# A hybrid RWKV-7 and pooling layer on one NeuronCore: some fp32 products of the time-mixing stage issued once per head, 64 stationary columns at a time

## The chip, the core and the metric

The kernel runs as one program on one core of a Trainium2 chip. The metric is device time in microseconds (us), the median of three runs. TensorE's clock has two levels, 1.2 and 2.4 GHz; the profile shows which one was granted.

Two things about the rows need saying once. A matrix product on TensorE is a pair of instructions: LDWEIGHTS puts the stationary operand into the array (PEld in the profile), MATMUL streams the moving operand past it (PE). And a product of two fp32 operands stands in the trace as two such pairs, so four products read "x8" on PE and "x8" on PEld; a product of two fp32r operands, and a transpose, stands as one pair. In a row, `128*128 128x64` means 128 active rows times 128 active (stationary) columns, and a moving operand of 64 columns; `128*64` would be 64 stationary columns. Column counts that repeat "128x" at the front count partitions first.

## The reference, cut to what matters

The layer normalises x, projects it with one large matrix, mixes the result over time in two branches, gates and merges them, projects again and adds an embedding. The change lies in branch A, the RWKV-7 recurrence of 16 heads of width 64, for a prompt of 256 tokens and 8 sample sequences of 8 tokens:

```python
def _wkv7_scan(S0, r, decay, k, v, a_vec, b_vec):
    # S_t = S_{t-1} diag(w_t) + (S_{t-1} a_t) b_t^T + v_t k_t^T ;  o_t = S_t r_t
    def step(S, inp):
        r_t, w_t, k_t, v_t, a_t, b_t = inp
        sa = jnp.einsum('bhij,bhj->bhi', S, a_t)
        S = S * w_t[..., None, :] + sa[..., :, None] * b_t[..., None, :] + v_t[..., :, None] * k_t[..., None, :]
        o = jnp.einsum('bhij,bhj->bhi', S, r_t)
        return S, o
...
    h = _rmsnorm(x, lw['norm_pre'])
    z = h @ lw['w_in']
...
    S, o = _wkv7_scan(wkv0, rh, decay.reshape(B, T, H, N), kh, vh, -kk, kk * ah)
...
    m = jax.nn.sigmoid(gate_a) * (y_a @ lw['w_branch'][0]) + jax.nn.sigmoid(gate_b) * (y_b @ lw['w_branch'][1])
    x = x + _rmsnorm(m @ lw['w_out'], lw['norm_post'])
    x = x + jax.nn.sigmoid(x @ lw['w_ple_gate']) * (p.astype(x.dtype) @ lw['w_ple'])
```

## The kernel before, in words

All 320 tokens (256 of the prompt, 64 of the samples) lie along the free dimension; channels lie on the 128 partitions. Every large weight matrix is split into a high and a low fp32r part (`wh`, `wl`, made by ACT and DVE from `wraw`), and each tile of 128 channels is made by `passes`: three products, wh by high, wh by low, wl by high, each with 320 or 328 moving columns. These are the rows of L1727, L1728 and L1729, in what follows the **stream**.

The recurrence is worked in 8 pairs of heads. A pair fills the 128 partitions, head 0 on rows 0 to 63 and head 1 on rows 64 to 127. The tokens are cut into G = 5 chunks of C = 64: four of the prompt (GP = 4), and one that holds the eight sample sequences. In a chunk the recurrence is a set of 64 by 64 matrix products for each head. To do both heads at once, the stationary operand is block diagonal: a tile such as `ABD`, `vBD` (also called `XBD`), `VtBD`, `kBD` (`SBD`) or `bBD` (`UBD`) holds for each chunk 128 columns, columns 0 to 63 with head 0's block on rows 0 to 63 and zeros below, columns 64 to 127 with head 1's block on rows 64 to 127 and zeros above. `flat(t, g)` gives these 128 columns.

`mix(r, q)` does the recurrence of pair r and, between its steps, the stream of pair q. `st.advance(n)` issues n steps of the stream (three products each), so that TensorE works while DVE, ACT and POOL prepare the next operand; the numbers in `AFTER` set by hand how many steps stand after which product. In the order of the program a pair's own products are:

- **sample states** (L1863): 8 products, one for each sample sequence, stationary `S0T`, moving `zr` with 80 columns;
- **scores** (L1869, L1874): 10 products with 128 moving columns, stationary `bBD` and `kBD`;
- `turned_keys`: 8 transposes;
- **inverse levels**, twice: `products(n)` (L1882: 4 products, stationary `ABD`, moving `Y`, 64 columns), three stream steps, `update(n)` (L1889: 4 products, stationary `XBD`, moving `Tm`, 64 columns), two stream steps. DVE masks the first result into `Tm`, and adds the second to `Y`;
- the **chain** over the four prompt chunks (L1915 to L1934), in which every product waits for DVE's result of the one before;
- **outputs** (L1945 to L1950): for each of the 5 chunks two or three products into one PSUM region, 14 in all, with 64 moving columns, and no stream between them; then a transpose, two wide products (L1958, L1959) and the mean (L1963).

Semaphores order the engines. The last product of each group tells the reader (`z_ps`, `t_ps`, `m_ps`, `o_ps`).

Of the kernel before, what the change touches and what calls it, by code (L numbers as in the profile page):

```python
# [30 lines left out]
P = 128  # L31
# [7 lines left out]
TB = 8  # L39
T = TP + NB * TB  # L40
TS = T + NB
C = 64
# [128 lines left out]
def build(nc, x_prompt, x_sample, state_wkv, state_shift, state_pool, p_prompt, p_sample, norm_pre, norm_post,  # L171
# [3 lines left out]
    with ExitStack() as ctx:  # L175
# [4 lines left out]
        def at(word, name, shape, dt=F32):  # L180
            size = int(np.prod(shape[1:])) * (2 if dt == BF16 else 4)
            used[name] = (word, word + (size + 3) // 4)
            return nc.alloc_sbuf_tensor_at(name, list(shape), dt, offset=base + 4 * word)
# [62 lines left out]
        ABD = r1.take("ABD", [P, G, 2, C])  # L246
# [4 lines left out]
        VtBD = r1.take("VtBD", [P, G, 2, C])  # L251
        ZaBD = r1.take("ZaBD", [P, 2, C])
        EndBD = r1.take("EndBD", [P, 2, C])
        S0T = r1.take("S0T", [P, NB, P])
        S0n = r1.take("S0n", [P, NB, C])
        S0D = r1.take("S0D", [P, NB, C])
        UBD, SBD, XBD = bBD, kBD, vBD
# [12 lines left out]
        ar = r1.take("ar", [P, 2, T])  # L270
        Y = r1.take("Y", [P, G, C])
        Tm = r1.take("Tm", [P, G, C])
        ARB = r1.take("ARB", [P, G, C])
        ARK = r1.take("ARK", [P, G, C])
# [6 lines left out]
        Zs = r1.take("Zs", [P, 2, C])  # L281
# [6 lines left out]
        zr = at(used["Y"][0], "zr", [P, NB, 2 * TB + C])  # L288
# [101 lines left out]
        x1h = at(used["hh"][0], "x1h", [P, KT * T], F32R)  # L390
        x1l = at(used["hl"][0], "x1l", [P, KT * T], F32R)
        end = max(b for _, b in used.values())
        room = (nc.sbuf_usable_end if not callable(nc.sbuf_usable_end) else nc.sbuf_usable_end())
        assert base + 4 * end <= room, (base + 4 * end, room)
# [5 lines left out]
        B01, B23, B45 = [ctx.enter_context(nc.psum_tensor(f"wide{i}", [P, 1024], F32)) for i in range(3)]  # L400
        B = [w[:, 512 * i:512 * (i + 1)] for w in (B01, B23, B45) for i in range(2)]
# [19 lines left out]
        def cfs(name):  # L421
            a, b = CF[name]
            return cf[:, a:b]
# [5 lines left out]
        ident, istk, ones2, meand = [cfs(n) for n in ("ident", "istk", "ones2", "meand")]  # L429

        def half(q):
            return slice(HD * q, HD * q + HD)
# [5 lines left out]
        def flat(t, g):  # L438

            return t[:, g].rearrange("p h c -> p (h c)")  # L440

        def tok(g):
            return slice(C * g, C * g + C)
# [1277 lines left out]
        def _(pe):  # L1721
            M = nc.tensor
# [21 lines left out]
            def transpose(out, in_):  # L1744
                rows = in_.shape[0]
                return M.transpose(out, in_, ident[0:rows, 0:rows])  # L1746


            pe.wait_ge(s["const_in"], 16)
            for _ in range(WARM):  # L1750
# [3 lines left out]
            for t in range(3):  # L1754
# [8 lines left out]
                for c in range(4):  # L1763
                    if t:
                        pe.wait_ge(s["hT_done"], 4 * (t - 1) + c + 1)
                    for k in range(4):
                        col = P * (4 * c + k)
                        last = M.matmul(B[c][:, P * k:P * k + n], rows_of[:, col:col + P], scales[0:n, t - 1, 0:n],
                                        start=True, stop=True) if t else transpose(B[c][:, P * k:P * k + n], rows_of[:, col:col + P])
# [46 lines left out]
            for j in range(1, CH_FIRST):  # L1816
# [8 lines left out]
                for n in [2 * k + m for k in MAP_TILES[j] for m in range(2)]:  # L1825
# [3 lines left out]
                             start=k == 0, stop=k == KT - 1).then_inc(s["xw_used"], 1)  # L1829
# [18 lines left out]
            def mix(r, q):  # L1848
# [11 lines left out]
                pe.wait_ge(s["dpl_ready"], r + 1)  # L1860
                pe.wait_ge(s["s0t_ready"], r * 2 + 2)
                for b in range(NB):
                    last = M.matmul(B45[:, P * b:P * b + 2 * TB + C], S0T[:, b, :], zr[:, b, :], start=True, stop=True)  # L1863
                last.then_inc(s["z_ps"], 1)

                pe.wait_ge(s["bbd_ready"], r * 2 + 2)
# [1 line left out]
                for g in range(G):  # L1868
                    last = M.matmul(B01[:, P * g:P * (g + 1)].rearrange("p (a c) -> p a c", a=2), flat(bBD, g),  # L1869
                                    ar[:, :, tok(g)], start=True, stop=True)  # L1870
                last.then_inc(s["score_ps"], 1)
                pe.wait_ge(s["bv_ready"], r + 1)
                for g in range(G):
                    last = M.matmul(B23[:, P * g:P * (g + 1)].rearrange("p (a c) -> p a c", a=2), flat(kBD, g),  # L1874
                                    ar[:, :, tok(g)], start=True, stop=True)
# [3 lines left out]
                def products(n):  # L1879
                    pe.wait_ge(s["y_ready"], r * (LEVELS + 1) + n + 1)  # L1880
                    for g in range(GP):
                        last = M.matmul(B[0][:, tok(g)], flat(ABD, g), Y[:, g, :], start=True, stop=True)  # L1882
                    last.then_inc(s["t_ps"], 1)

                def update(n):
                    pe.wait_ge(s["t_ready"], r * LEVELS + n + 1)
                    pe.wait_ge(s["x_ready"], r * (2 * LEVELS) + 2 * n + 2)
                    for g in range(GP):
                        last = M.matmul(B[1][:, tok(g)], flat(XBD, g), Tm[:, g, :], start=True, stop=True)  # L1889
                    last.then_inc(s["m_ps"], 1)  # L1890

                def turned_keys():
# [7 lines left out]
                for n in range(LEVELS):  # L1900
                    pe.wait_ge(s["ark_ready"], r * 5 + (3 if n == 0 else 5))
                    products(n)
                    st.advance(AFTER["product"])
                    update(n)
                    st.advance(AFTER["update"])
# [4 lines left out]
                for n in range(2):  # L1910
                    last = transpose(B[5][:, P * n:P * (n + 1)], tail4[:, n].rearrange("p h c -> p (h c)"))
                last.then_inc(s["tail_ps"], 1)

                for g in range(GP):
                    M.matmul(B[2][:, 0:C], flat(AKBD, g), Vs[:, g, :], start=True, stop=g == 0)  # L1915
                    if g == 0:
                        M.matmul(B[2][:, C:2 * C], flat(AKBD, G - 1), Vs[:, G - 1, :], start=True, stop=False)
                        last = M.matmul(B[2][:, C:2 * C], ZaBD[:, :, :].rearrange("p h c -> p (h c)"), istk, start=False, stop=True)
                    else:
                        pe.wait_ge(s["s_ready"], r * GP + g)  # L1920
                        last = M.matmul(B[2][:, 0:C], flat(aBD, g), Ss[:, g - 1, :], start=False, stop=True)
# [5 lines left out]
                    last = M.matmul(B[3][:, 0:C], flat(YBD, g), RHS[:, 0, :], start=True, stop=True)  # L1927
                    if g == 0:
                        last = M.matmul(B[3][:, C:2 * C], flat(YBD, G - 1), RHS[:, 1, :], start=True, stop=True)
# [11 lines left out]
                for g in range(G):  # L1941
                    if g == 1:
                        pe.wait_ge(s["sbd_ready"], r * 2 + 2)
                    o = B[4][:, tok(g)]
                    M.matmul(o, flat(VtBD, g), ARK[:, g, :], start=True, stop=False)  # L1945
                    if g == G - 1:
                        M.matmul(o, ident, Zs[:, 1, :], start=False, stop=False)
                    elif g:
                        M.matmul(o, flat(SBD, g - 1), ar[:, 1, tok(g)], start=False, stop=False)
                    last = M.matmul(o, flat(UBD, g), ARB[:, g, :], start=False, stop=True)  # L1950
                last.then_inc(s["o_ps"], 1)

                pe.wait_ge(s["endbd_ready"], r * 2 + 2)
# [29 lines left out]
            with pe.Fori(1, PAIRS) as q:  # L1983
                mix(q - 1, q)
            mix(PAIRS - 1, PAIRS)


# [35 lines left out]
            for k in range(8):  # L2023
                w = NB * BUF
                last = transpose(B[k // 4][:, w * (k % 4):w * (k % 4 + 1)], spt[:, P * k:P * (k + 1)])
# [151 lines left out]
```

## Time and profile before

| | us |
|---|---|
| median of 3 runs (range) | 1162.03 (1160.96 to 1163.07) |
| the profiled execution, its span | 1162.2 |
| TensorE busy with matmuls / with weight loads | 1143.0 / 1113.6 |
| VectorE (DVE) busy | 815.9 |
| ScalarE (ACT) busy | 524.9 |
| one pair of heads in the steady part | 63.9 |

The span is the time from the first to the last instruction of one profiled execution. A busy matmul row is not the time that a matmul costs: matmuls are pipelined, each row runs from its start until its results are out, and rows overlap. What a matmul costs is read from the starts: the distance from the start of one group to the start of the next. The first matmul of a stream after an fp32 group is shown starting early, while its weights are still loading: its distance to the next start is 0.23 us, where 0.147 is the rule; the 0.08 us between them belongs to the group before.

### The profile page before, as it was taken

What the parts mean: (1) busy time and instruction counts of PE and PEld (TensorE: products, weight loads), DVE (VectorE), ACT (ScalarE), POOL (GpSimd) and SP (SyncE); (2) the same over time, 40 slices, a digit from 0 to 9 for tenths busy, and PEclk for the clock granted to TensorE, in tenths of its full rate; (3) what the DMA queues carried; (4) which work ended last, traced back from release to release, by engine and by line L of the source; (5) the groups of instructions that cost most, each with busy time, mean ns of one, the idle gap of its engine ahead of it and who ended that gap; (6) DMA issues with size and microseconds to landing.
All of it is one profiled execution on the core that took longest, in us unless ns stands there. A gap on an engine that the chain in (4) does not pass through costs nothing.

```text
span 1162.2 us, 22008 instructions
## 1 busy us (share of the span) xinstructions
PE 1143.0 (98%) x7826; PEld 1113.6 (96%) x7826; DVE 815.9 (70%) x1727; ACT 524.9 (45%) x888; POOL 148.9 (13%) x251
## 2 busy tenths in 40 slices
PE   6999999999999999999999999999999999999998
PEld 6889999999999999999999999999999999989998
DVE  5979898889898898988679644444444487775442
ACT  5444645546474636455363333333333243354332
POOL 2322131204031121211050000000000500000000
PEclk9999999999999999999999999999999999999999
DMA  9714433434334334343464555545555975515551
GB/s 242 189 37 122 119 103 112 109 108 113 108 101 120 100 103 118 103 114 97 118 184 126 157 152 144 147 142 162 144 146 156 259 196 156 148 56 158 161 163 42
DMA packets 279707, 155.08 MB, mean 133 GB/s; under 512 B 7717, under 2 KB 275661, under 8 KB 279012
## 3 DMA queue, kind: packets, MB, share of 16 engines
q1 hardware_dynamic: 272528, 139.65, 43.2%
q0 software_dynamic: 6992, 14.87, 5.1%
q8 instruction: 25, 0.41, 0.2%
q14 instruction: 14, 0.11, 0.0%
q10 hardware_dynamic: 148, 0.04, 0.0%
HBM read 149.15 MB, written 5.61 MB: 133 GB/s over the span
## 4 chain that ended last, share of the span: by engine, by line
PE 89%; DVE 5%; DMA 3%; issue 2%; ACT 1%; SPq 0%; DVEq 0%; ACTq 0%
PE acc L1727 19%; PE acc L1728 18%; PE acc L1729 18%; PE wide L1729 5%; PE wide L1728 5%; PE wide L1727 5%; DVE wl L1085 2%; PE wide L1828 2%; PE wide L2112 1%; PE wide L1746 1%; DMA wraw<-in_w_out 1%; PE wide L1882 1%; PE wide L1863 1%; PE wide L1950 1%; DMA xt<-in_x_prompt 1%
## 5 line engine op out<-in xcount | busy, mean ns | idle before, releaser
L1085 DVE TENSOR_TENSOR wl<-wraw,wh 128x1024 fp32r<-128x1024 f32 x256 | 317.6, 1249 | 167.0 <-ACT wh L709 164.6
L709 ACT CAST wh<-wraw 128x1024 fp32r<-128x1024 f32 x256 | 266.9, 1048 | 217.8 <-PE acc L1729 125.7
L1727 PE MATMUL acc<-hh,wh 128*128 128x320 f32 (+1 forms) x1084 | 348.9, 322 | 2.4 <-DVE hl L1171 1.9
L1728 PE MATMUL acc<-hl,wh 128*128 128x320 f32 (+1 forms) x1084 | 336.5, 310 | 0.0
L1729 PE MATMUL acc<-hh,wl 128*128 128x320 f32 (+1 forms) x1084 | 335.9, 310 | 0.0
L1727 PEld LDWEIGHTS acc<-hh,wh 128*128 128x128 f32 x1084 | 204.4, 189 | 3.7 <-DVE hl L1171 2.4
L1728 PEld LDWEIGHTS acc<-hl,wh 128*128 128x128 f32 x1084 | 204.1, 188 | 0.3
L1729 PEld LDWEIGHTS acc<-hh,wl 128*128 128x128 f32 x1084 | 204.0, 188 | 0.0
L1727 PE MATMUL acc<-x1h,wh 128*128 128x320 f32 x256 | 81.0, 316 | 0.0
L1727 PE MATMUL acc<-mh,wh 128*128 128x320 f32 x256 | 79.4, 310 | 1.5 <-DVE wl L1085 1.5
L1729 PE MATMUL acc<-x1h,wl 128*128 128x320 f32 x256 | 79.1, 309 | 0.0
L1729 PE MATMUL acc<-mh,wl 128*128 128x320 f32 x256 | 79.1, 309 | 0.0
L1728 PE MATMUL acc<-ml,wh 128*128 128x320 f32 x256 | 79.1, 309 | 0.0
L1728 PE MATMUL acc<-x1l,wh 128*128 128x320 f32 x256 | 79.1, 309 | 0.0
L1729 PE MATMUL wide<-hh,wl 128*128 128x320 f32 x192 | 59.5, 310 | 0.0
L1728 PE MATMUL wide<-hl,wh 128*128 128x320 f32 x192 | 59.3, 309 | 0.0
L1727 PE MATMUL wide<-hh,wh 128*128 128x320 f32 x192 | 59.2, 308 | 0.0
L1727 PEld LDWEIGHTS acc<-mh,wh 128*128 128x128 f32 x256 | 48.1, 188 | 1.9 <-DVE wl L1085 1.8
L1728 PEld LDWEIGHTS acc<-x1l,wh 128*128 128x128 f32 x256 | 48.1, 188 | 0.2
L1727 PEld LDWEIGHTS acc<-x1h,wh 128*128 128x128 f32 x256 | 48.1, 188 | 0.2
L1728 PEld LDWEIGHTS acc<-ml,wh 128*128 128x128 f32 x256 | 48.1, 188 | 0.0
L1729 PEld LDWEIGHTS acc<-mh,wl 128*128 128x128 f32 x256 | 48.1, 188 | 0.0
(424 smaller groups left out, 2099.5 us busy)
## 6 DMA issues: line engine op xcount, KB each, us to landing
wraw<-in_w_in SPq DMA_DIRECT2D x160, 512.0 KB, 3.8
wraw<-in_w_branch SPq DMA_DIRECT2D x32, 512.0 KB, 3.9
wraw<-in_w_out SPq DMA_DIRECT2D x32, 512.0 KB, 4.6
wraw<-in_w_ple_gate SPq DMA_DIRECT2D x32, 512.0 KB, 4.1
xt<-in_x_prompt SPq DMA_DIRECT2D x2, 1024.0 KB, 6.8
S0n<-in_state_wkv POOLq DMA_DIRECT2D x64, 32.0 KB, 4.3
out<-so POOLq DMA_DIRECT2D x16, 128.0 KB, 3.6
xt<-in_x_prompt POOLq DMA_DIRECT2D x2, 1024.0 KB, 8.6
```

What stands on the lines that cost most here:

```text
L709: A.copy(wh[:, slot, :], wraw[:, slot, :]).then_inc(s["hi_ready"], 1)
L1085: V.tensor_tensor(wl[:, slot, :], wraw[:, slot, :], wh[:, slot, :].bitcast(F32), ALU.subtract).then_inc(s["lo_ready"], 1)
L1727: M.matmul(out[:, 0:width], wh[:, slot, wcol], hi, start=first, stop=False)
L1728: M.matmul(out[:, 0:width], wh[:, slot, wcol], lo, start=False, stop=False)
L1729: return M.matmul(out[:, 0:width], wl[:, slot, wcol], hi, start=False, stop=last)
L1746: return M.transpose(out, in_, ident[0:rows, 0:rows])
L1828: M.matmul(B[n % 2][0:RANK, 0:T], (lw1, la1)[n % 2][:, k, :], xw[:, n % 4, :], start=k == 0, stop=k == KT - 1).then_inc(s["xw_used"], 1)
L1863: last = M.matmul(B45[:, P * b:P * b + 2 * TB + C], S0T[:, b, :], zr[:, b, :], start=True, stop=True)
L1882: last = M.matmul(B[0][:, tok(g)], flat(ABD, g), Y[:, g, :], start=True, stop=True)
L1950: last = M.matmul(o, flat(UBD, g), ARB[:, g, :], start=False, stop=True)
L2112: last = M.matmul(B[i % 4][:, 0:T], embedding_weights(i)[:, P * k:P * (k + 1)], pT[:, k, :], start=k == 0, stop=k == 1)
```

## The change

A helper, `by_head`, issues a product as two: head 0's 64 stationary columns into PSUM partitions 0 to 63, then head 1's 64 columns into partitions 64 to 127, both with the same moving operand. It takes the place of the plain product for the sample states, both kinds of inverse-level products, and the outputs. The scores, the transposes, the chain, the wide products and the stream stay as they are. Waits and signals stay where they were; a group's signal goes with the last half of the last product.

```diff
+            def by_head(out, heads, rhs, start, stop):
+
+                for h in range(2):
+                    last = M.matmul(out[half(h)], heads[:, half(h)], rhs, start=start, stop=stop)
+                return last
...
-                    last = M.matmul(B45[:, P * b:P * b + 2 * TB + C], S0T[:, b, :], zr[:, b, :], start=True, stop=True)
+                    last = by_head(B45[:, P * b:P * b + 2 * TB + C], S0T[:, b, :], zr[:, b, :], True, True)
...
-                        last = M.matmul(B[0][:, tok(g)], flat(ABD, g), Y[:, g, :], start=True, stop=True)
+                        last = by_head(B[0][:, tok(g)], flat(ABD, g), Y[:, g, :], True, True)
...
-                        last = M.matmul(B[1][:, tok(g)], flat(XBD, g), Tm[:, g, :], start=True, stop=True)
+                        last = by_head(B[1][:, tok(g)], flat(XBD, g), Tm[:, g, :], True, True)
...
-                    M.matmul(o, flat(VtBD, g), ARK[:, g, :], start=True, stop=False)
+                    by_head(o, flat(VtBD, g), ARK[:, g, :], True, False)
                     if g == G - 1:
-                        M.matmul(o, ident, Zs[:, 1, :], start=False, stop=False)
+                        by_head(o, ident, Zs[:, 1, :], False, False)
                     elif g:
-                        M.matmul(o, flat(SBD, g - 1), ar[:, 1, tok(g)], start=False, stop=False)
-                    last = M.matmul(o, flat(UBD, g), ARB[:, g, :], start=False, stop=True)
+                        by_head(o, flat(SBD, g - 1), ar[:, 1, tok(g)], False, False)
+                    last = by_head(o, flat(UBD, g), ARB[:, g, :], False, True)
```

In the built program each half carries a tile of 128 rows by 64 columns of the array, at column 0 for head 0 and at column 64 for head 1; every plain product around it carries the whole array, 128 by 128. No instruction moves past another; DVE, ACT and SP have the same order as before.

On TensorE, around the first inverse level of a pair (`Y`, `Tm`, `ABD`, `vBD` as above, `acc<-` the stream, `cf` the identity of a transpose), before:

```order
L1746 MATMUL wide<-cf,kBD 128x128 x4
L1901 ISA
L1882 MATMUL wide<-Y,ABD 128x64 x4
L1727 MATMUL acc<-hh,wh 128x320
L1728 MATMUL acc<-hl,wh 128x320
```

and now:

```order
L1746 MATMUL wide<-cf,kBD 128x128 x4
L1907 ISA
L1751 MATMUL wide<-Y,ABD 64x64 x8
L1727 MATMUL acc<-hh,wh 128x320
L1728 MATMUL acc<-hl,wh 128x320
```

The four products became eight halves at the same place, between whole-array transposes and the whole-array stream.

On TensorE, at the start of a pair's outputs (`VtBD`, `bBD`, `kBD` stationary), before:

```order
L1729 MATMUL acc<-hh,wl 128x320
L1945 MATMUL wide<-ARK,VtBD 128x64
L1950 MATMUL wide<-ARB,bBD 128x64
L1945 MATMUL wide<-ARK,VtBD 128x64
L1949 MATMUL wide<-ar,kBD 128x64
L1950 MATMUL wide<-ARB,bBD 128x64
```

and now:

```order
L1729 MATMUL acc<-hh,wl 128x320
L1751 MATMUL wide<-ARK,VtBD 64x64 x2
L1751 MATMUL wide<-ARB,bBD 64x64 x2
L1751 MATMUL wide<-ARK,VtBD 64x64 x2
L1751 MATMUL wide<-ar,kBD 64x64 x2
L1751 MATMUL wide<-ARB,bBD 64x64 x2
```

Each product became two halves behind each other; the groups of one chunk still follow each other without anything between.

## Rows read from the trace of the kernel before

**Rows 1.** The page: busy times, the granted clock, the chain that ended last.

```profile
PE 1143.0 (98%) x7826; PEld 1113.6 (96%) x7826; DVE 815.9 (70%) x1727; ACT 524.9 (45%) x888; POOL 148.9 (13%) x251
...
PEclk9999999999999999999999999999999999999999
...
PE 89%; DVE 5%; DMA 3%; issue 2%; ACT 1%; SPq 0%; DVEq 0%; ACTq 0%
```

**Rows 2.** Who TensorE waited for, whole span: total us, times, longest.

```profile
PE wide L1746 <- DMA cf<-in_const_f: 6.4, 1, 6.4
PE wide L1746 <- DVE scales L1135: 2.7, 1, 2.7
PE acc L1727 <- DVE wl L1085: 2.1, 2, 1.5
```

**Rows 3.** Busy time of each engine in one pair; columns as the header says.

```profile
core 0: us, PE busy (x) PEld busy (x) DVE busy (x) ACT busy (x) POOL busy (x), PEclk, DMA share, GB/s
...
171.80:235.70 63.90, 63.81 (x460) 62.41 (x459) 55.77 (x156) 35.24 (x69) 11.97 (x21) 1.00 0.40 109
```

**Rows 4.** Timeline of TensorE in one pair: the first update between two streams.

```profile
493.30 0.31 PE L1729 MATMUL acc<-hh,wl 128*128 128x320 f32 x1
493.45 1.00 PE L1889 MATMUL wide<-Tm,vBD 128*128 128x64 f32 x8
494.26 0.39 PE L1727 MATMUL acc<-hh,wh 128*128 128x320 f32 x1
494.49 0.31 PE L1728 MATMUL acc<-hl,wh 128*128 128x320 f32 x1
```

**Rows 5.** Timeline of TensorE: second and last output product of a pair, then the wide ones.

```profile
512.80 0.39 PE L1950 MATMUL wide<-ARB,bBD 128*128 128x64 f32 x2
...
515.48 0.39 PE L1950 MATMUL wide<-ARB,bBD 128*128 128x64 f32 x2
...
515.82 1.02 PE L1958 MATMUL wide<-xpB,bBD 128*128 128x512 f32 x2
516.68 1.02 PE L1959 MATMUL wide<-xpK,VtBD 128*128 128x512 f32 x2
```

**Rows 6.** Timeline of TensorE: the sample states and the scores.

```profile
472.48 1.91 PE L1863 MATMUL wide<-zr,S0T 128*128 128x80 f32 x16
474.22 1.32 PE L1869 MATMUL wide<-ar,bBD 128*128 128x128 f32 x10
475.38 1.28 PE L1874 MATMUL wide<-ar,kBD 128*128 128x128 f32 x10
```

**Rows 7.** Weight loads by shape, whole span: busy us, mean ns.

```profile
L1882 PEld LDWEIGHTS wide<-Y,ABD 128*128 128x128 f32 x128 | 15.5, 191 | 3.1 <-DVE Y L1433 2.6 <-issue 0.5
...
L1828 PEld LDWEIGHTS wide<-xw,la 128*96 128x96 f32 x32 | 5.2, 163 | 3.4 <-DVE xw L1214 0.2
```

**Rows 8.** Timeline of TensorE: transposes, the last from 64 rows (row tile 64 by 128).

```profile
1006.13 0.59 PE L1746 MATMUL wide<-cf,pt 128*128 128x128 f32 x3
1006.65 0.41 PE L1727 MATMUL acc<-mh,wh 128*128 128x320 f32 x1
1006.90 0.31 PE L1728 MATMUL acc<-ml,wh 128*128 128x320 f32 x1
```

**Rows 9.** Timeline of TensorE: transposes, the last with 64 stationary columns.

```profile
1075.39 0.49 PE L1746 MATMUL wide<-cf,yo 128*128 128x128 f32 x3
1075.64 0.39 PE L1727 MATMUL acc<-x1h,wh 128*128 128x320 f32 x1
1075.87 0.31 PE L1728 MATMUL acc<-x1l,wh 128*128 128x320 f32 x1
```

**Rows 10.** Matmuls by shape, whole span: the third transposes of rows 8 and 9.

```profile
L1746 PE MATMUL wide<-cf,yo 128*64 128x128 f32 x16 | 4.4, 272 | 0.0
...
L1746 PE MATMUL wide<-cf,pt 64*128 64x64 f32 x2 | 0.6, 275 | 0.0
```

## The prediction

> **What bounds the kernel now.** I read the page first: TensorE has a matmul in flight for 1143.0 us of 1162.2, at the higher clock level (2.4 GHz) throughout, and the chain that ended last lies for 89% on it [rows 1]. Then who TensorE waited for: after 9 us of start-up loads the longest item is 2.1 us for split weights [rows 2]. Then one pair of heads in the steady part: of 63.9 us TensorE is busy 63.81, DVE 55.77, ACT 35.24 [rows 3]. So TensorE's own instruction stream sets the end, and each us cut from it comes off the time, as long as DVE's 55.8 us a pair stay below the pair's new length. The profiled span is 1162.2 us, the median 1162.03: the sum can be made against either.
>
> What must be read next is what limits TensorE inside the products that change. Busy rows don't say it, starts do. The update's four products: their start to the next stream row is 0.81 us, and that stream row is early by 0.08 (0.23 to its successor instead of 0.147), so 0.89 us, or 0.223 each [rows 4]. The outputs: 2.68 us from the second to the fourteenth product, twelve products, again 0.223 each [rows 5]. The sample states, 80 moving columns instead of 64: 1.74 us for eight, 0.218 [rows 6]. A product is two pairs of load and matmul, so a pair takes 0.112 us, and it is the same for 64 and for 80 moving columns. The matmul does not set it. Its streaming time is seen where it is long: the wide products with 512 columns start 0.86 us apart, 0.43 for one of the two matmuls, 0.84 ns a column [rows 5]; that makes 0.054 us for 64 columns and 0.067 for 80. What sets 0.112 us is the weight load of 128 columns; half of the time the array streams nothing.
>
> **The change part by part.** *Count.* A pair has 8 products of sample states, 16 of inverse levels, 14 of outputs: 38, in six groups (one, four, one). Before they cost 38 x 0.223 = 8.47 us a pair, 67.8 us for eight pairs. All of it lies on TensorE's path; nothing hides it.
>
> *A load of 64 columns.* Loads of 128 columns take 191 ns in the rows, of 96 columns 163: 0.875 ns a column [rows 7]. 64 columns less make the load 0.056 us shorter: 0.112 becomes 0.056. The half load is then as long as the 64-column stream. There are twice as many: four loads of 0.056 and four matmuls of 0.054 a product.
>
> *Side by side or in turn.* That is the open term, and the trace of before has no two neighbouring column tiles at work to show it. The bounds: if the two heads' halves, which sit in different columns of the array, load and stream beside each other, a product takes two loads, 0.112 us, and two streams of 0.067 = 0.134 for the sample states. If they go in turn it takes four loads, 0.224, and 4 x 0.067 = 0.268 for the sample states. I take side by side, with a little for matmuls starting one after another: 0.12 and 0.14. My reason is that the heads share neither columns nor output partitions, and that load and stream already overlap in the rows. A pair then costs 30 x 0.12 + 8 x 0.14 = 4.72 us: 3.75 less.
>
> The Trainium skill says the same of column tiles ("TensorEngine Tiling (Array Packing)", Tiling Modes, Key Properties: different tiles can load weights and multiply in parallel); no row of before shows it. By that statement the gain before switching costs is the 3.75 us a pair above; without it, nothing.
>
> *Entering and leaving the half-width tile.* Each group now stands between whole-array instructions, so six times a pair the array's division changes and changes back. One row pair shows such a change: three transposes, the last a tile of 64 rows, take from 1006.13 to 1006.90 up to the stream's second row [rows 8, 10]; three others, the last with 64 stationary columns, take from 1075.39 to 1075.87 [rows 9, 10]. 0.77 against 0.48: the row tile costs 0.29 us in and out, the narrow transpose nothing. The bounds for a group are 0 and 0.29. The narrow transpose looks nearer by shape, but it is a transpose that the array may handle whole, so I lean on the other: loads wait for the matmul before to come out. The entering load is 0.056 us shorter than there, so I take 0.25: 6 x 0.25 = 1.5 us a pair.
>
> The same section of the Trainium skill says that a change of the tiling mode drains TensorE; the row-tile row agrees with its 0.29 us, the 64-column row shows none. With a drain the gain is 2.25 us a pair, without it 3.75.
>
> *The sum.* 3.75 - 1.5 = 2.25 us a pair, 18 us for eight pairs: 1162 - 18 = **1144 us**.
>
> *What else moves.* Nothing in order. The masks and sums by DVE between the levels start from a group's last matmul and are covered by the same three or two stream steps; cover and waits shift as a whole. Next late would be DVE: a pair of 61.65 us against 55.8 of DVE work leaves room [rows 3], and even 60.15 would. The scores keep 128 columns: 1.16 us for ten matmuls of 128 columns, 0.116, where streaming them takes 0.107, so halves would have brought nothing there [rows 6]. More instructions, 76 additional matmuls and as many loads a pair, must also be issued; I see no sign that issue is near, and price it with the last rival.
>
> **The rivals.** *Side by side, and the change of tile is free* (the 64-column transpose is right): -3.75 x 8 = -30 us, 1132.
>
> *In turn, with the change of tile at its price*: this is the slower side. One mechanism: the array has one path for weights, so loads of the two heads follow each other. Place: every one of the six groups. Price: 30 x (0.224 - 0.223) + 8 x (0.268 - 0.223) + 1.5 to 1.74, so 1.9 to 2.1 us a pair, and a nanosecond or two on each of 152 loads adds 0.2: 2.2 x 8 = +17.5, 1179.5. For it: the load path already is what these products wait for, and two heads don't add a second one by themselves. The point from which it decides: a product over 0.18 us on average eats the gain, since 38 x (0.223 - 0.183) = 1.5 us.
>
> *In turn, free change*: +0.4 us a pair, +3: 1165.
>
> *Partly side by side*: streams beside each other, loads mostly in turn, about 0.17 us a product: -2.0 + 1.5 us a pair, 1158; it could as well come out at 1162.
>
> *Load and stream take turns in a half-width tile, or issue limits them to about the same*: each half pair costs 0.056 + 0.054, a product 0.44: +0.217 x 38 + 1.5 = 9.7 us a pair, 1240. The Trainium skill has a rule that would do this ("TensorE: Matmul & The Clock Gate", Part 3, The mechanism: a weight load overlaps matmuls in flight only when the row group differs); the halves share their row group. The trace speaks against it as it stands: load and stream in turn would make 0.112 + 0.054 = 0.166 a pair where the rows show 0.112 [rows 4]. So it gets a small chance.
>
> **How the numbers follow.** Side by side with the change paid 0.38 (1144); side by side and free 0.13 (1132); partly 0.10 (1158); in turn and free 0.09 (1165); in turn and paid 0.24 (1179.5); load and stream in turn 0.06 (1240). The first is likeliest; its own range is 1138 to 1150. The measurement can tell 0.2%, 2.3 us, from no change. Faster by more: 0.38 + 0.13 + 0.03 of the partly case = 0.54. Same: 0.04 of the partly case and 0.03 of the free one = 0.07. Slower: the rest, 0.39. A range that holds 8 in 10 must take in both sides: 1131 to 1181 leaves out the last rival and the tails of the outer cases.
>
> **What would show it.** In the changed profile, read the starts. The update's rows should show 0.12 us a product within the group and about 0.1 us of nothing on each side; the outputs should shrink from 3.07 us to about 2.0, the sample states from 1.8 to about 1.4; the pair from 63.9 to about 61.6. If matmuls of the second head start 0.05 us after the first's, beside each other fails, and the outputs take 3.4. If there is no gap where a group meets the stream, the free change is right. If DVE's wait for TensorE vanishes and TensorE begins to wait for `wl`, DVE has become the bound, and the gain was cut there. The prediction is wrong altogether if a product takes over 0.18 us.

## The result: 1155.37 us, and where the time went

The changed kernel takes 1155.37 us (median of 4 runs, 1153.43 to 1157.9), the kernel before 1162.55 (4 runs, 1160.96 to 1164.91). The ratio is 0.9942, 95% interval 0.9928 to 0.9956: faster by 7 us. The forecast was faster by 18 us, with a range of 1131 to 1181. The direction and the range held; the size was off by more than a factor of two.

The page of the changed kernel first: busy times, and the chain that ended last.

```profile
PE 1129.7 (98%) x8434; PEld 1087.0 (94%) x8434; DVE 814.5 (71%) x1727; ACT 524.3 (45%) x888; POOL 146.7 (13%) x251
...
PE 86%; DVE 7%; DMA 3%; issue 2%; ACT 1%; SPq 0%; DVEq 0%; ACTq 0%
```

Beside [rows 1] two things stand out: 608 more matmuls (7826 to 8434: 76 for each of 8 pairs), and the chain lies 7% on DVE where it lay 5%. The clock was granted in full again. So some of TensorE's time has been cut, and some of what was cut is spent waiting for DVE.

One update of a pair, TensorE's timeline, the same place as [rows 4]:

```profile
488.77 0.31 PE L1729 MATMUL acc<-hh,wl 128*128 128x320 f32 x1
489.01 0.69 PE L1751 MATMUL wide<-Tm,vBD 128*64 128x64 f32 x16
489.62 0.41 PE L1727 MATMUL acc<-hh,wh 128*128 128x320 f32 x1
489.88 0.31 PE L1728 MATMUL acc<-hl,wh 128*128 128x320 f32 x1
```

From the last stream row to the second one after the group it was 1.19 us [rows 4] and is 1.11: 0.08 us gained on four products. The gap on the left is new: the half-width group starts 0.24 us after the last stream matmul, where 0.147 is the stream's own step.

A pair's outputs, the same place as [rows 5] (first, second and last output product, then the wide products and the mean):

```profile
507.78 0.34 PE L1751 MATMUL wide<-ARK,VtBD 128*64 128x64 f32 x4
507.95 0.29 PE L1751 MATMUL wide<-ARB,bBD 128*64 128x64 f32 x4
...
509.35 0.29 PE L1751 MATMUL wide<-ARB,bBD 128*64 128x64 f32 x4
509.56 0.33 PE L1746 MATMUL wide<-cf,EndBD 128*128 128x128 f32 x1
...
509.73 1.02 PE L1964 MATMUL wide<-xpB,bBD 128*128 128x512 f32 x2
510.59 1.02 PE L1965 MATMUL wide<-xpK,VtBD 128*128 128x512 f32 x2
...
512.46 0.42 PE L1969 MATMUL wide<-O_h,dev_r 128*128 128x320 f32 x1 [0.85 <-DVE O_l L1472]
```

Twelve products from the second to the last take 1.40 us, 0.117 each, against 0.223. That is two heads side by side. But the last line waits: the mean's first matmul comes 1.87 us after the second wide product where it came 0.72 us after it (517.40 in the trace of before, 516.68 in [rows 5]). 1.15 us is what the outputs had gained. Who TensorE waited for, whole span, says the same:

```profile
PE wide L1969 <- DVE O_l L1472: 5.9, 7, 0.8
...
PE acc L1727 <- DVE wl L1085: 1.1, 2, 0.6
```

The line on `O_l` is not in the list of before, of which [rows 2] are the longest items. Seven pairs wait for it; the eighth has no next pair whose work stands ahead of it on DVE. The list counts only time in which no matmul row is still running, 5.9 us; by the starts the seven waits cost 7.8 us.

The pair itself went from 63.87 to 63.01 us (distance between the starts of two pairs' sample states). By place, in us, from the starts of the groups: sample states -0.34 (with the entry and the exit), the four inverse-level groups -0.49, outputs -1.15, the wait before the mean +1.11. The sum is -0.87. Eight times the first three and seven times the wait make -8.1; the two profiled spans differ by 7.9 us (1162.2 and 1154.3), the medians by 7.2.

### The profile page after: what moved, and what is told of

Same layout as the page of the kernel before. It is cut to its first block, busy times and chain, and to the rows that moved or that the text cites. A ratio compares the mean times of both kernels' runs of the same rounds, so it can differ in the third digit from the quotient of the medians.

```text
span 1154.3 us, 23224 instructions
## 1 busy us (share of the span) xinstructions
PE 1129.7 (98%) x8434; PEld 1087.0 (94%) x8434; DVE 814.5 (71%) x1727; ACT 524.3 (45%) x888; POOL 146.7 (13%) x251
## 4 chain that ended last, share of the span: by engine, by line
PE 86%; DVE 7%; DMA 3%; issue 2%; ACT 1%; SPq 0%; DVEq 0%; ACTq 0%
PE acc L1727 19%; PE acc L1728 18%; PE acc L1729 18%; PE wide L1729 5%; PE wide L1728 5%; PE wide L1727 5%; PE wide L1751 3%; DVE wl L1085 2%; PE wide L1834 2%; PE wide L2118 1%; PE wide L1746 1%; DMA wraw<-in_w_out 1%; PE wide L1875 1%; DMA xt<-in_x_prompt 1%; PE wide L2017 1%
## 5 line engine op out<-in xcount | busy, mean ns | idle before, releaser
L1729 PEld LDWEIGHTS acc<-x1h,wl 128*128 128x128 f32 x256 | 48.0, 188 | 0.0
```

Source lines behind the costliest of these rows:

```text
L1729: return M.matmul(out[:, 0:width], wl[:, slot, wcol], hi, start=False, stop=last)
```

## Why DVE was late: its own queue

DVE's timeline between the end of the chain and `O_l`, in the kernel before:

```profile
511.58 0.28 DVE L1461 SCALAR_TENSOR_TENSOR Ss<-wide,pd,Sd 128x64 f32<-128x64 f32 x1
...
515.32 1.22 DVE L1085 TENSOR_TENSOR wl<-wraw,wh 128x1024 fp32r<-128x1024 f32 x1
516.46 0.48 DVE L1109 COPY uS<-acc 128x320 f32 x1
516.86 0.48 DVE L1472 TENSOR_TENSOR O_l<-wide,O_h 128x320 fp32r<-128x320 f32 x1
```

and in the changed kernel:

```profile
506.64 0.28 DVE L1461 SCALAR_TENSOR_TENSOR Ss<-wide,pd,Sd 128x64 f32<-128x64 f32 x1
...
510.38 1.23 DVE L1085 TENSOR_TENSOR wl<-wraw,wh 128x1024 fp32r<-128x1024 f32 x1
511.52 0.48 DVE L1109 COPY uS<-acc 128x320 f32 x1
511.93 0.48 DVE L1472 TENSOR_TENSOR O_l<-wide,O_h 128x320 fp32r<-128x320 f32 x1
512.32 2.14 DVE L1192 RECIPROCAL rn<-rn 128x320 f32<-128x320 f32 x1
```

From the chain's last `Ss` to `O_l` it is 5.28 us in the one and 5.29 in the other. DVE works through a fixed queue there (a weight split, the next pair's low parts and transposes, another split, a copy) and is not idle. Before, TensorE needed about the same time for its three stream steps, the outputs and the wide products, so the two paths ran level, and the list of TensorE's waits shows nothing of it. The list of what the weight loads waited for, in the kernel before, does: the mean's load waits in each of the eight pairs, behind the wide products that are still running.

```profile
PEld wide L1963 <- DVE O_l L1472: 3.9, 8, 0.5
```

Theory A, then: in this stretch DVE's queue is the bound as soon as TensorE gets faster, and the halved outputs bring nothing. Theory B, the rival: the outputs do bring their 1.15 us, and the shortfall is the changes of tile, six a pair, dearer than I had put them.

## Experiments on the outputs

**Outputs whole again, the rest halved (e1).**

```diff
-                    by_head(o, flat(VtBD, g), ARK[:, g, :], True, False)
+                    M.matmul(o, flat(VtBD, g), ARK[:, g, :], start=True, stop=False)
...
-                    last = by_head(o, flat(UBD, g), ARB[:, g, :], False, True)
+                    last = M.matmul(o, flat(UBD, g), ARB[:, g, :], start=False, stop=True)
```

> The changed kernel with the 14 output products of a pair put back to 128 stationary columns; sample states and inverse levels stay halved. Theory A (the outputs' gain is swallowed: from the end of the chain to O_l it is DVE's queue that sets the time, 6.36 us in both profiles, and TensorE then waits 1.15 us a pair before the mean): a pair takes 63.05 us, the time stays within 1 us of the changed kernel, about 1156, and the wait before the mean is gone. Rival B (the shortfall against the forecast is spread over the changes of tile, and the outputs do bring their 1.15 us a pair): a pair takes 64.2 us, the time is about 1164.6.

Measured: 1156.7 us (1155.24 to 1157.41, 5 runs), ratio to before 0.9947 (0.9934 to 0.996); a pair takes 63.05 us. The wait for `O_l` is gone from the list. Theory A, by the pair and by the wait; the median lies 1.3 us above the changed kernel's, and the two ratios' intervals overlap.

**Only the outputs halved, the rest as before (e2).**

> The kernel before with only the output products halved. Theory A: TensorE finishes the outputs 1.2 us earlier a pair and waits 1.1 us before the mean instead; a pair takes 63.8 us against 63.87, the time is 1162, no change that can be measured. Rival B: 62.7 us a pair, about 1153.

Measured: 1161.56 us (12 runs), ratio 0.9987 (0.9979 to 0.9996); a pair takes 63.83 us. The outputs shrink from 3.07 to 1.78 us on TensorE, and the wait stands in their place, as in the changed kernel:

```profile
PE wide L1969 <- DVE O_l L1472: 5.9, 7, 0.8
```

Fourteen of 38 products, over half of what TensorE gains net (1.15 of 1.98 us a pair), are worth 0.04 us a pair, 0.3 in eight pairs; the medians differ by 1.3 us (1162.85 for the kernel before in this batch), and where the other 1.0 comes from is not shown. As the reason for the whole shortfall theory B is out; how much dearer the changes of tile are is worked out below.

**`O_l` ahead of the split and the copy on DVE (e3).** If the queue is the bound, its order should matter. In the changed kernel:

```diff
-                go(10)
-                out(4)
                 dve.wait_ge(s["o_ready"], r + 1)
                 V.tensor_tensor(O_l[:, :], B[4][:, 0:T], O_h[:, :].bitcast(F32), ALU.subtract).then_inc(s["sum_lo"], 1)
+                go(10)
+                out(4)
```

> The changed kernel with DVE's O_l put ahead of the weight split and the copy of uS that stood before it in DVE's queue. Theory A: O_l is ready 1.5 us earlier, the wait of 1.15 us a pair before the mean goes, a pair takes 61.9 to 62.1 us, the time is about 1147. Rival C (DVE is simply full: the split that moves behind O_l comes late, and TensorE waits for wl or for a free accumulator instead): half of it or less, 1151 to 1155, with TensorE waiting for wl L1085 or uS.

Measured: 1154.92 us (5 runs), ratio 0.9933 (0.992 to 0.9946); 62.90 us a pair. My number was a miss. The rival's range of 1151 to 1155 took the time in, but not its sign: TensorE waits neither for `wl` nor for the copy more than it did. It waits for the next low part:

```profile
PE wide L1973 <- DVE dsq_l L1477: 5.1, 7, 0.7
```

The wait before the mean is gone, and the 15 stream matmuls between mean and variance take 3.11 us instead of 2.21, because the variance now stands waiting behind them. What I had called the end of the DVE-bound stretch was its middle: behind `O_l` stands the reciprocal of 2.14 us, and then `dsq_l`. Nothing had been taken off the queue, so its end came no earlier.

**The same move in the kernel before (e4).**

> The kernel before with the same move of O_l on DVE, nothing halved. Theory A: before, TensorE came to the mean only 0.1 us too early, so the move brings at most 0.14 us a pair: 1161 to 1162.5. Rival D (the move itself is what brings time, halves or not): 1155 or less.

Measured: 1170.02 us (5 runs), ratio 1.006 (1.0047 to 1.0073): slower by 7 us, which neither theory had. The outputs come late there, and DVE, with `O_l` at the head of its queue, stands idle for them; the list of who DVE waited for:

```profile
DVE O_l L1470 <- ACT O_h L904: 11.1, 8, 3.5
```

A pair takes 64.8 us, 0.9 more, and the pair pays at `dsq_l` for what DVE has idled. So in this stretch DVE is the bound in the kernel before too, or within the 0.04 us of e2.

**Both low parts early (e10).** The move of `O_l` as above, and the reciprocal behind `dsq_l`:

```diff
-                if more:
-                    key_inverse(q, rn[:, :])
                 dve.wait_ge(s["dsq_ready"], r * 2 + 2)
                 V.tensor_tensor(dsq_l[:, :], dsq[:, :], dsq_h[:, :].bitcast(F32), ALU.subtract).then_inc(s["sum_lo"], 1)
+                if more:
+                    key_inverse(q, rn[:, :])
```

> As e3 (O_l before the weight split and the copy on DVE), and the reciprocal rn of 2.14 us moved behind dsq_l, so that neither low part that TensorE waits for stands behind other work. Theory A2 (DVE's queue from the end of the chain to dsq_l is the bound; e3 only moved the wait of 1.15 us from the mean to the variance, S15 3.11 us instead of 2.21): both waits go, a pair takes 61.8 to 62.0 us, the time is about 1146.5. Rival C2 (DVE's total work between the chain's end and the next pair's keys is the bound, in whatever order): the wait moves on, to the bonus sum or the sample states, and a pair stays over 62.7 us, 1153 or more.

Measured: 1149.69 us (4 runs), ratio 0.9892 (0.9877 to 0.9907); 61.97 to 62.21 us a pair in the steady part, so 3 us more than the expected 1146.5 in all. Both waits are gone. A smaller one, 0.5 us in all in the changed kernel, has grown at the inverse levels:

```profile
PE wide L1751 <- DVE Y L1433: 2.1, 6, 0.6
```

**Stream steps ahead of the wait (e11).** Instead of moving DVE's work, give TensorE something to do: three of the pair's 96 stream steps before the wait for `O_l`, three fewer at the pair's end.

```diff
+                st.advance(3)
                 pe.wait_ge(s["sum_lo"], r * 3 + 2)
                 M.matmul(B[5][:, 0:T], dev_r[:, :], O_h[:, :], start=True, stop=False)
```

> The changed kernel with three of the pair's stream steps (1.32 us) issued before the wait for O_l instead of at the end of the pair; DVE's order as in the changed kernel. Theory A2: the 1.15 us that TensorE waited are filled, the bonus sum had 2.2 us to spare at the other end: 61.9 us a pair, about 1146.5. Rival C2: the wait moves on to the bonus sum; 62.7 us a pair or more, 1153.

Measured: 1147.69 us (1147.23 to 1148.34, 4 runs), ratio 0.9877 (0.9862 to 0.9892); 61.90 us a pair. The wait for `O_l` is not in the list any more. One line of code brings 7.7 us more, as much again as the change itself, and this is the fastest kernel of the case.

**The two controls.** The same three steps in the kernel before (e14):

> The kernel before with the same three stream steps issued before the wait for O_l, nothing halved. Theory A2: TensorE waited there hardly at all (0.1 us a pair), so no more than 1 us of the span: 1161.5 to 1163.5. Rival D2 (the moved stream steps bring time by themselves): 1155 or less.

Measured: 1162.15 us (11 runs), ratio 0.9996 (0.9987 to 1.0005); 63.87 us a pair. So the steps bring nothing by themselves; they free what the halves had gained. And e10 with whole outputs (e12):

> e10 with the output products back at 128 columns. Theory A2: if e10 has taken the bound away from DVE, the halved outputs are now worth their 1.15 us a pair on TensorE, so this one is slower than e10 by up to 9 us, unless O_l, now first in DVE's queue, makes DVE wait for the later outputs as in e4 (then slower still). Rival (outputs bring nothing in any arrangement): the same as e10.

Measured: 1158.86 us (7 runs), ratio 0.9974 (0.9963 to 0.9985), 9.2 us slower than e10. DVE idles for the late outputs here as in e4:

```profile
DVE O_l L1470 <- ACT O_h L904: 11.0, 8, 3.5
```

But this time TensorE doesn't pay for it. Its list of waits has neither `O_l` nor `dsq_l`, and from the mean's start to the variance's it is 2.91 us, against 2.92 in e10. The difference lies in the outputs themselves: from the start of the three stream steps ahead of them to the first wide product it is 4.59 us against 3.44. With the bound taken off DVE the halved outputs are worth what TensorE's rows say, 1.15 us a pair. The stream steps in the changed kernel give the same picture: a wait of 1.11 us in each of seven pairs is 7.8 us, and 7.7 were measured.

## Experiments on the halves themselves

**One head after the other (e6).** Same instructions in another order, in sample states and levels:

```diff
-                    for g in range(GP):
-                        last = by_head(B[1][:, tok(g)], flat(XBD, g), Tm[:, g, :], True, True)
+                    for h in range(2):
+                        for g in range(GP):
+                            last = M.matmul(B[1][half(h), tok(g)], flat(XBD, g)[:, half(h)], Tm[:, g, :], start=True, stop=True)
```

> The changed kernel with the halves of sample states and inverse levels in another order: all of head 0's, then all of head 1's; same instructions, same number. If two heads go beside each other only when they stand next to each other in the queue, each half goes at its own 0.112 us, a product costs 0.224 again and a pair 24 x 0.107 = 2.6 us more: 65.6 us, about 1176. Rival (TensorE reaches far enough ahead in its queue to pair them anyway): no change, 1155.4.

Measured: 1169.32 us (4 runs), ratio 1.0062 (1.0047 to 1.0077); 64.86 us a pair. The gain comes from two column tiles at work beside each other, and that needs them near each other in the queue. An update in this kernel, TensorE's timeline:

```profile
370.54 0.97 PE L1898 MATMUL wide<-Tm,vBD 128*64 128x64 f32 x16
371.44 0.41 PE L1727 MATMUL acc<-hh,wh 128*128 128x320 f32 x1
```

0.90 us instead of 0.61. I had expected 1.04, four products at 0.107 more each. The single starts in the trace show why it is less: head 0's eight loads start 0.055 to 0.059 us apart from 370.54 on, and head 1's first starts at 370.83, beside head 0's sixth. Head 0 is alone for five such steps, and these are the 0.29 us. In the sample states, where head 0 has 16 loads, head 1's first starts beside the fourteenth. So the engine does reach a few instructions ahead, past head 0's last two loads, but not eight. Both theories had a part of it.

**More changes of tile (e7).** Every other sample-state product whole:

```diff
+                    one = M.matmul if b % 2 else by_head
-                    last = by_head(B45[:, P * b:P * b + 2 * TB + C], S0T[:, b, :], zr[:, b, :], True, True)
+                    last = one(B45[:, P * b:P * b + 2 * TB + C], S0T[:, b, :], zr[:, b, :], start=True, stop=True)
```

> The changed kernel with every other one of the 8 sample-state products put back to 128 columns, so that the array's division changes 8 times in that group instead of twice. If a change costs about 0.17 us wherever it stands: 6 x 0.17 + 4 x 0.08 = 1.3 us a pair more, 64.3 us, about 1166. Rival (only the meeting with the long fp32r stream costs): 0.3 us a pair more, about 1158.

Measured: 1164.19 us (10 runs), ratio 1.0015 (1.0004 to 1.0026); 64.27 us a pair, 1.26 more than the changed kernel. The timeline of TensorE at this place:

```profile
343.93 0.36 PE L1751 MATMUL wide<-zr,S0T 128*64 128x80 f32 x4
344.22 0.45 PE L1870 MATMUL wide<-zr,S0T 128*128 128x80 f32 x2
344.59 0.36 PE L1751 MATMUL wide<-zr,S0T 128*64 128x80 f32 x4
```

A halved and a whole product together take 0.67 us (344.59 - 343.93 = 0.66, and the next two the same); without changes they are 0.145 + 0.223 = 0.37. Two changes cost 0.30, one 0.15: 0.29 - 0.145 from the halved product to the whole one, 0.37 - 0.22 back. Around a group in the stream it is about the same, 0.34 for the two (below).

**The chain halved too (e8)**, each of its 22 products by `by_head`, in 12 groups of one to three:

> The changed kernel with the chain's products halved too: 22 products in 12 groups of one to three. At 0.34 us in and out of the half-width tile for a group and 0.107 us gained on a product: 12 x 0.34 - 22 x 0.107 = +1.7 us a pair, 64.7 us, about 1169. Rival (what counts in the chain is the latency of a product, which is shorter in halves): faster than the changed kernel.

Measured: 1167.69 us (4 runs), ratio 1.0046 (1.0031 to 1.0061); 64.38 us a pair, 1.37 more than the changed kernel, where 1.7 was expected. TensorE's own cost is nearer to it: the wait before the mean shrank by 0.24 us. By these figures (an estimate) a group pays from the fourth product on: three gain 0.32 us, the change in and out costs 0.30 to 0.34.

**The scores halved too (e5)**, 10 products with 128 moving columns:

> The changed kernel with the 10 score products (128 moving columns) halved as well, so that sample states and scores are one half-width stretch. Two streams of 0.107 us a head, beside each other, make 0.214 us a product where 0.223 to 0.232 stand now: 0.1 to 0.2 us a pair less, 62.85 us, time about 1154.3, not to be told from the changed kernel. Rival (halves overlap worse where the stream is the longer part): 0.25 or more a product, 0.2 us a pair slower or worse, 1157 and up.

Measured: 1155.13 us (6 runs), ratio 0.9942 (0.9931 to 0.9954); 62.97 us a pair against 63.01. Two streams of 0.109 us beside each other make 0.218 us a product, nearly the 0.223 that one whole product costs. No gain, no loss that can be measured.

## Why the prediction was right in sign and wrong in size

- *What a product costs is the load of 128 columns* (0.112 us a load): right. With half the columns and two heads beside each other it is 0.117 us a product; 0.12 was forecast, 0.14 for 80 columns, 0.145 measured (the sample states of e5, 1.158 us for eight).
- *Side by side*: right. e6 shows it, and its price when it is lost.
- *Entering and leaving the half-width tile*, forecast 0.25 us a group: **mis-sized**. Around an update the stream-to-stream time less the products is 1.19 - 0.89 = 0.30 before and 1.11 - 0.47 = 0.64 after, so 0.34; e7 gives 0.30 between fp32 products. The row tile's 0.29 of [rows 8] was the right neighbour and should have been taken whole; taking off the shorter load was wrong. The 64-column transpose of [rows 9] was no evidence for a free change. Over the pair the faster products alone would give 30 x 0.106 + 8 x (0.218 - 0.145) = 3.76 us, as forecast (3.75), and 1.98 came of it; so the six groups cost 1.78 us (0.24 at the sample states, 0.30 at a level, 0.33 at the outputs) instead of 1.5: 0.28 us a pair, 2.2 us in all. The Trainium skill ("TensorEngine Tiling (Array Packing)", Tiling Modes, Key Properties) says that a change of the tiling mode drains TensorE; these rows agree with it, at 0.15 us a change. The same section of the Trainium skill says that different tiles load and multiply in parallel; the 0.117 us a product agrees. The Trainium skill also says ("TensorE: Matmul & The Clock Gate", Part 3, The mechanism) that a weight load overlaps matmuls in flight only when the row group differs. That doesn't hold here: in e6 load and stream of head 0 alone, in the same rows of the array, come every 0.058 us, where by the estimates from [rows 5, 7] the load takes 0.056 and the stream 0.054.
- *What else moves*: **this step failed**. I wrote that all of the products' cost lies on TensorE's path, that cover and waits shift as a whole, and that DVE had room because a pair has 55.8 us of DVE work in 61.65. A mean over the pair says nothing on a stretch. From the chain's end to `O_l` DVE works without a gap for 5.3 us, and at the mean TensorE could come only 0.04 us earlier (e2). The outputs' gain came to lie exactly there: 1.11 of 1.15 us a pair, 7.8 us in seven pairs, was turned into a wait. The trace of before had the sign, in the 3.9 us that the mean's load waited; I had gone by the matmuls' list alone. e1 and e2 show that it is lost, e11 gives it back. I had named the sign to look for (DVE the bound, the gain cut there), but looked for it at `wl`, and gave it no chance and no price. At the inverse levels the phrase held: ahead of the second level TensorE waited for `Y` before (six stream matmuls take 1.22 us there, where 0.96 would do) and still does (1.19), but that wait runs from the update's last matmul on and so moved forward with it.
- With e11 the sum can be closed: 63.87 - 61.90 = 1.97 us a pair on TensorE against the 2.25 forecast. The difference is the 0.28 us that the changes of tile cost more. In all: 18 - 7.8 - 2.2 = 8.0 us, where the spans differ by 7.9.
- *That the time lies in the range* is no merit of the mechanism. The range was made wide for heads in turn, which did not happen (0.117 us a product), and the nearest case, "partly side by side" at 1158, gives about this time by another cause.

What stays open: why one change costs 0.15 us was only seen, not taken apart; and whether e10's wait for `Y` comes from the reciprocal that now stands later was not tried (e12 has the same order on DVE and the same 2.1 us).

## What to carry to other kernels

Before you book a gain on the engine that bounds the whole, look at the place where it falls: list what the other engines do between the last thing that they get from this engine and the next thing that they give it. If that queue has no gaps and the engine already comes to the hand-over with nothing to spare, the gain becomes a wait, whatever the averages say; and then a few steps of independent work ahead of the wait can be worth as much as the speed-up was (7.7 us here, after 7.2). Read the waits of the weight loads as well as those of the matmuls. Halving the stationary columns pays for fp32 products that are short in moving columns (64 or 80 here, not 128), if the halves alternate between the column tiles and at least four products stand together.

## What the runs showed of the hardware

- Two column tiles of 64 with neighbouring instructions load and multiply beside each other: an fp32 product with 64 moving columns goes from 0.223 to 0.117 us. With eight load and matmul pairs of one tile ahead of the other's, the second tile's first load starts only beside the sixth, with sixteen beside the fourteenth (e6).
- Changing between the whole array and half-width tiles costs 0.15 us each way (e7), and the next load starts only when the matmul before is nearly out: at the update above the group's first load starts at 489.01, where the stream's last matmul ends at 489.08, and the stream's first load at 489.62, where the group's matmuls end at 489.70.
- I had not expected that moving one small DVE instruction forward could cost 7 us (e4): it made DVE idle in a stretch where it had no time to spare.
